# The last scaling and addition of a two-block kernel, shared between GpSimd and the vector engine, with the output stored in 768 and 256 KB

## The chip, the core and the metric

The kernel runs on one core of a Trainium2 chip. The metric is the device time of one execution in microseconds; the numbers given are the median of several executions. Besides the times there is one execution taken by the hardware profiler, with a page and a trace of it.

## What is computed

Two transformer-like blocks follow each other on a sequence of 256 tokens with 1024 features. The change touches only the last statement of the second block's second layer: the merged result `out` is normalised over its features, multiplied by a gain and a gate, and added to the residual `x`, which is then the result of the whole program.

```python
def rms_norm(x, g=None):
    xf = x.astype(jnp.float32)
    y = xf * lax.rsqrt(jnp.mean(xf * xf, axis=-1, keepdims=True) + EPS)
    if g is not None:
        y = y * g.astype(jnp.float32)
    return y.astype(x.dtype)

def second_block(x, c, ctx, c_ctx, w_mod, ...):
    ...
    for l in range(DEPTH_2):
        ...
        out = merge_branches(o_ret, o_mlp, o_diff, mlog_, w_branch_out[l], w_out[l])
        x = x + gate * rms_norm(out, g_post[l])
        ...
    return x
```

## The kernel before

All activations stand with the features on the 128 partitions. The residual is `h`, 8 tiles (`KT`) of 128 features by 256 tokens (`T`) in float32, 1 MB in all and 1 KB of each partition per tile. The weights come as a stream of units of 512 KB through a ring of four buffers, loaded by the queue of SyncE (`sp`, line 511 and, for the last three, line 514). ScalarE (`act`) makes the high part of a unit (line 1319), the vector engine (`dve`) the low part (line 468, `w_lo` = `ring` minus `w_hi`), and TensorE (`pe`) multiplies by both. Nothing is scheduled automatically: each engine's program is written out in order, and the engines wait for each other by counting semaphores.

The end of the program, which is what the change touches, runs as follows.

- For each of the 8 output tiles of the last product (`wo`), ScalarE squares the tile into `sq2` (line 1887) and writes the tile, scaled by the gate, into `unnormed` (line 1874; `unnormed` is a name for `diffz`, and `area` in the trace). The vector engine folds the squares together (line 1915), and TensorE sums them over the partitions (line 576).
- ScalarE turns the sum into `rstd`, 128 x 256, by a logarithm and an exponential (lines 1307 and 1308). The exponential raises the semaphore `out_rstd`, which the vector engine waits for.
- `add_out` (from line 2345) then works on pairs of tiles, 128 x 512 elements each. Line 2353 multiplies a pair of `unnormed` by `rstd`, repeated over the two tiles, and line 2356 adds the pair to `h`. The two kinds are interleaved, so that an addition never waits for the multiplication just before it: multiply 0, multiply 1, add 0, multiply 2, add 1, multiply 3, add 2, add 3. Each addition raises `resid_ready` by 2.
- SyncE stores `h[:, 0:4]` once two pairs are added (line 516), and `h[:, 4:8]` once all four are (line 518), 512 KB each. It then waits for both stores, and all engines meet at the end of the program (line 233).

GpSimd (`pool`) does a few small jobs earlier. Its last are the multiplications of line 2776, 128 x 256, in the middle of the second layer. It also runs the additions of line 2763, 128 x 512. Its helper `link` raises `pool_step` and waits for it, that is, it lets an instruction finish before the next one starts. The semaphore `pool_laid` has been raised three times by other lines of GpSimd before the end.

Of the kernel before, what the change touches and what calls it, by code (L numbers as in the profile page):

```python
# [14 lines left out]
ALU = mybir.AluOpType  # L15
# [6 lines left out]
P = 128  # L22
AREA = 25472
D = 1024
KT = D // P
T = 256
# [14 lines left out]
LAYERS = 2  # L41
# [144 lines left out]
RESID_BLOCK2 = 4 + 4 + KT + KT  # L186
# [18 lines left out]
def slot_units(l):  # L205

    return [(part, l, j) for part in SLOT_PARTS[l] for j in range(4)]
# [24 lines left out]
def two_block_kernel(nc, stream, mod_stream, cond, pack, pack2, bs_rows, x_in, ctx_in, out):  # L232
    with ExitStack() as es:
        def sb(name, shape, dt=F32):
            return es.enter_context(nc.sbuf_tensor(name, shape, dt))

        def sem(name):
            return es.enter_context(nc.semaphore(name))
# [13 lines left out]
        h = sb("h", [P, KT, T])  # L252
# [15 lines left out]
        rstd = sb("rstd", [P, 2 * T])  # L268
# [19 lines left out]
        def cut(*shape):  # L288
            n = int(np.prod(shape))
            v = area[:, Area.at:Area.at + n]  # L290
            Area.at += n
            if len(shape) == 2:
                v = v.rearrange("p (a b) -> p a b", a=shape[0])
            if len(shape) == 3:
                v = v.rearrange("p (a b c) -> p a b c", a=shape[0], b=shape[1])
            return v
# [59 lines left out]
        sp = cut(4, 16)  # L356
# [3 lines left out]
        def early_swapped(part, l):  # L360

            at = 2 + 2 * EARLY_ROPES[l].index(part)
            return aux[:, at:at + 2, :].rearrange("p a b -> p (a b)").rearrange("p (a b) -> p a b", b=T)

        def swaps(part):

            half = HD // 2 if part[0] == "d" else HD
            return [(to, to + half if to // half % 2 == 0 else to - half, half) for to in range(0, P, half)]
# [31 lines left out]
        unnormed = diffz  # L400
# [26 lines left out]
        resid_ready = sem("resid_ready")  # L427
# [3 lines left out]
        stored = sem("stored")  # L431
        S = {}

        def s(name):
            if name not in S:
                S[name] = sem(name)
            return S[name]
# [3 lines left out]
        def wait_taken(eng, name):  # L441

            _, _, who, count = BANK[name]
            eng.wait_ge(EV[who], count)
# [25 lines left out]
        def load_mod(eng, m, body=0, first=False):  # L470

            if not first:
                eng.wait_ge(s("mod_used"), m - 1 + body)
            eng.dma_start(mod_slot(m), mod_stream[m + body]).then_inc(s(f"mod_loaded{m % 2}"), 16)
# [20 lines left out]
        @block.sync  # L495
        def _(sp):
            sp.dma_start(h[:, :, :], x_in).then_inc(consts_loaded, 16)
            sp.dma_start(pk[:, 0:width(PACK)], pack[:, 0:width(PACK)]).then_inc(consts_loaded, 16)
            for u in range(RING):
                sp.dma_start(ring[:, u, PLACE:], stream[u]).then_inc(unit_loaded[u], 16)  # L500
            sp.dma_start(pk[:, width(PACK):width(PACK + PACK1)], pack[:, width(PACK):]).then_inc(block1_loaded, 16)
            for st in range(2):
                sp.dma_start(cond_silu(st), cond[:, st]).then_inc(s("cond_loaded"), 16)
            for m in range(2):
                load_mod(sp, m, first=True)
            rounds = NU // RING
            with sp.Fori(1, rounds) as r:
                for u in range(RING):

                    sp.wait_ge(units_multiplied, RING * r + (u + 1 - RING))  # L510
                    sp.dma_start(ring[:, u, PLACE:], stream[RING * r + u]).then_inc(unit_loaded[u], 16)
            for u in range(rounds * RING, NU):
                sp.wait_ge(units_multiplied, u + 1 - RING)
                sp.dma_start(ring[:, u % RING, PLACE:], stream[u]).then_inc(unit_loaded[u % RING], 16)
            sp.wait_ge(resid_ready, RESID_BLOCK2 + LAYERS * KT - KT // 2)
            sp.dma_start(out[:, 0:KT // 2, :], h[:, 0:KT // 2, :]).then_inc(stored, 16)
            sp.wait_ge(resid_ready, RESID_BLOCK2 + LAYERS * KT)
            sp.dma_start(out[:, KT // 2:KT, :], h[:, KT // 2:KT, :]).then_inc(stored, 16)
            sp.wait_ge(stored, 32)


# [1380 lines left out]
        def _(dve):  # L1902
# [8 lines left out]
            tt_, ts, stt = dve.tensor_tensor, dve.tensor_scalar, dve.scalar_tensor_tensor  # L1911
# [433 lines left out]
            def add_out(l, st, x, done, tiles):  # L2345

                before = outs_scaled[0] - tiles[0]
                outs_scaled[0] += len(tiles)
                v = slice(T * st, T * st + T)
                both = rstd[:, v].unsqueeze(1).broadcast_to([P, 2, T])  # L2350
                for k in range(tiles[0], tiles[0] + len(tiles) + 2, 2):
                    if k in tiles:
                        tt_(unnormed[:, k:k + 2, v], unnormed[:, k:k + 2, v], both, ALU.mult).then_inc(s("out_scaled"), 2)
                    if k - 2 in tiles:
                        dve.wait_ge(s("out_scaled"), before + k)
                        tt_(x[:, k - 2:k, :], x[:, k - 2:k, :], unnormed[:, k - 2:k, v], ALU.add).then_inc(done, 2)
# [133 lines left out]
            for l in range(LAYERS):  # L2490
# [178 lines left out]
                        fold(v, k, k - 1)  # L2669

                dve.wait_ge(s("out_rstd"), 1 + 2 * l)
                add_out(l, 0, h, resid_ready, range(KT))


        @block.gpsimd
        def _(pool):
# [8 lines left out]
            tt_, ts = pool.tensor_tensor, pool.tensor_scalar  # L2685
# [65 lines left out]
            def decay_tables(l, hh):  # L2751

                n = 4 * l + hh
                f, b = dmat[:, hh, :], aux[:, 9, :]
                three = lambda v: v.rearrange("p (a b) -> p a b", a=2)
                pool.wait_ge(s("decay_exp"), 2 * n + 1)
                link(pool.affine_select(out=three(f), in_=three(f), compare_op=ALU.is_ge, fill=0.0, base=0,
                                        pattern=[[-P, 2], [1, T]], channel_multiplier=-1))
                pool.wait_ge(s("decay_exp"), 2 * n + 2)
                pool.affine_select(out=three(b), in_=three(b), compare_op=ALU.is_ge, fill=0.0, base=0,  # L2760
                                   pattern=[[P, 2], [-1, T]], channel_multiplier=1).then_inc(s("decay_masked"), 1)
                pool.wait_ge(s("decay_masked"), 2 * n + 1)
                pool.tensor_tensor(f, f, b, ALU.add).then_inc(s("decay_masked"), 1)
# [20 lines left out]
            def swap_halves(part, l):  # L2784

                z, at = (diffz if part[0] == "d" else retz), (0 if part[1] == "k" else 4)
                dst = early_swapped(part, l) if part in EARLY_ROPES[l] else ring_swapped
                wait_taken(pool, (part, l, 3))
                for to, of, n in swaps(part):
                    pool.dma_start(dst[to:to + n, :, :], z[of:of + n, at:at + 4, 0:T]).then_inc(s(SWAPPED[part, l][0]), 16)  # L2790

            pool.wait_ge(block2_loaded, 16)
            for l in range(LAYERS):
                for part in EARLY_ROPES[l]:
                    if l == 1 and part == "dq":
                        pool.wait_ge(s("ctx_modulated"), LAYERS * KT)
                    swap_halves(part, l)
                for slot, name in enumerate(slot_units(l)):
                    for kind, step in SLOTS[l][slot]:
                        if kind == "tables":  # L2800
                            decay_tables(l, step)
                        if kind == "ret":
                            ret(l, step)
                    if name == ("rk", l, 3):
                        swap_halves("rk", l)
                    if name == ("rq", 0, 3):
                        pool.wait_ge(s("ring_roped"), RING_ROPED["rk", 0])
                        swap_halves("rq", l)

# [167 lines left out]
```

## Time and profile before

| what | us |
|---|---|
| median of 3 executions | 1491.61 |
| lowest and highest of them | 1489.47, 1491.94 |
| the profiled execution, its own time | 1491.69 |
| span of its trace | 1490.0 |

The profiled execution took 1.7 us more than the span of its trace, and it lies 0.08 us above the median. In the span TensorE was busy for 1445.0 us (97%), the vector engine for 957.8 us (64%), ScalarE for 721.5 us (48%) and GpSimd for 96.9 us (7%). These shares are means over a long program; the change lies in its last 8 us, where TensorE has already ended. So the end has to be read by itself, from the timeline and the chain of waits of the last microseconds.

### The profile page before, as it was taken

The page shows a single profiled execution, that of the slowest core. Times are in us where ns is not written, and L with a number is a line of the kernel's source. Part 1 is how long each engine was busy: PE and PEld are TensorE (multiplying, and loading weights), DVE is VectorE, ACT ScalarE, POOL GpSimd, SP SyncE. Part 2 cuts the span into 40 slices and gives each one's busy share as a digit, 9 for nine tenths or more (in the row PEclk, how much of TensorE's full clock was granted, in tenths as well). Part 3 has the DMA queues.
Part 4 walks back from the last instruction along what each step waited for, and adds up shares of the span by engine and source line. Part 5 has one row for each costly group of instructions (what it writes and reads, how often), then busy time and mean ns, then how long its engine had stood idle before and what let it go on. Part 6 is the DMA issues. An engine that isn't in the chain of part 4 may idle for free.

```text
span 1490.0 us, 25861 instructions
## 1 busy us (share of the span) xinstructions
PE 1445.0 (97%) x9976; PEld 1289.9 (87%) x9976; DVE 957.8 (64%) x1516; ACT 721.5 (48%) x1252; POOL 96.9 (7%) x153
## 2 busy tenths in 40 slices
PE   6999999989999999999999999999999999999997
PEld 6999999769999998877778788888889887889997
DVE  5888788677666678865654447654246745647665
ACT  5444466366444466336445353222245446556444
POOL 4700000000000000102001000000000103010000
PEclk9999999999999999999999999999999999999999
DMA  7766646516666644652222224533333542325663
GB/s 275 241 219 199 214 142 197 171 69 224 224 219 212 222 165 145 199 160 78 86 73 70 62 80 153 172 127 113 99 102 108 152 127 85 100 87 185 210 210 130
DMA packets 72440, 227.43 MB, mean 153 GB/s; under 512 B 7072, under 2 KB 21408, under 8 KB 71840
## 3 DMA queue, kind: packets, MB, share of 16 engines
q1 hardware_dynamic: 54528, 194.67, 40.4%
q10 hardware_dynamic: 16416, 27.34, 5.7%
q0 software_dynamic: 1408, 4.20, 1.2%
q8 instruction: 61, 1.00, 0.3%
q14 instruction: 27, 0.22, 0.1%
HBM read 220.94 MB, written 1.05 MB: 149 GB/s over the span
## 4 chain that ended last, share of the span: by engine, by line
PE 86%; DVE 5%; ACT 4%; DMA 3%; issue 2%; DVEq 0%; SPq 0%; ACTq 0%
PE ps L548 36%; PE ps L561 20%; PE ps L553 18%; DMA ring<-stream 2%; PE ps L576 2%; PE ps L1069 1%; ACT w_hi L1319 1%; PE ps L1085 1%; DVE w_lo L468 1%; PE ps L1077 1%; PE ps L1153 1%; PE ps L1142 1%; PE ps L1122 0%; DMA pk<-pack 0%; PE ps L1102 0%
## 5 line engine op out<-in xcount | busy, mean ns | idle before, releaser
L468 DVE TENSOR_TENSOR w_lo<-ring,w_hi 128x1024 fp32r<-128x1024 f32 (+1 forms) x347 | 414.7, 1201 | 269.0 <-ACT w_hi L1319 264.9
L1319 ACT ACTIVATE w_hi<-ring 128x1024 fp32r<-128x1024 f32 (+1 forms) x347 | 360.2, 1039 | 331.3 <-DMA ring<-stream 249.4
L548 PE MATMUL ps<-hn_hi,w_hi 128*128 128x256 f32 (+1 forms) x1720 | 494.7, 316 | 3.2 <-ACT area L1388 1.6
L548 PE MATMUL ps<-hn_lo,w_hi 128*128 128x256 f32 (+1 forms) x1720 | 486.2, 311 | 0.0
L548 PEld LDWEIGHTS ps<-hn_hi,w_hi 128*128 128x128 f32 x1720 | 324.3, 189 | 26.7 <-issue 5.6
L548 PEld LDWEIGHTS ps<-hn_lo,w_hi 128*128 128x128 f32 x1720 | 324.4, 189 | 19.3 <-issue 0.7
L553 PE MATMUL ps<-hn_hi,w_lo 128*128 128x256 f32 (+1 forms) x1720 | 291.8, 312 | 0.4 <-DVE w_lo L468 0.4
L553 PEld LDWEIGHTS ps<-hn_hi,w_lo 128*128 128x128 f32 x1720 | 247.5, 189 | 20.4 <-DVE w_lo L468 0.7
L1388 ACT ACTIVATE area<-ps 128x512 f32<-128x512 f32 (+1 forms) x136 | 67.1, 507 | 196.2 <-PE ps L553 182.2
L561 PE MATMUL ps<-area_r,w_hi 128*128 128x256 f32 (+1 forms) x578 | 131.8, 323 | 0.6 <-ACT area L1388 0.3
L561 PEld LDWEIGHTS ps<-area_r,w_hi 128*128 128x128 f32 x578 | 95.7, 188 | 10.7 <-DVE w_lo L468 0.9
L561 PE MATMUL ps<-area_r,w_lo 128*128 128x256 f32 (+1 forms) x289 | 92.6, 320 | 0.0
L548 PE MATMUL ps<-hid_hi,w_hi 128*128 128x256 f32 x352 | 83.0, 278 | 1.7 <-DVE hid_lo L2044 1.7
L548 PE MATMUL ps<-hid_lo,w_hi 128*128 128x256 f32 x352 | 82.6, 277 | 0.0
L561 PE MATMUL ps<-w_hi,hn_hi 128*128 128x512 f32 (+1 forms) x192 | 77.1, 402 | 0.0
L561 PE MATMUL ps<-w_lo,hn_hi 128*128 128x512 f32 (+1 forms) x192 | 73.4, 382 | 0.0
L561 PE MATMUL ps<-w_hi,hn_lo 128*128 128x512 f32 (+1 forms) x192 | 73.3, 382 | 0.0
L548 PEld LDWEIGHTS ps<-hid_hi,w_hi 128*128 128x128 f32 x352 | 66.1, 188 | 2.1 <-issue 1.0
L548 PEld LDWEIGHTS ps<-hid_lo,w_hi 128*128 128x128 f32 x352 | 66.3, 188 | 0.0
L561 PE MATMUL ps<-hn_hi,w_hi 128*128 128x256 f32 (+1 forms) x175 | 56.0, 320 | 5.0 <-DVE hn_lo L1926 2.9
L2790 POOL DMA_DIRECT2D area<-area x24 | 14.1, 595 | 686.3 <-ACT area L1388 686.3
L561 PEld LDWEIGHTS ps<-area_r,w_lo 128*128 128x128 f32 x289 | 54.3, 188 | 4.5
(331 smaller groups left out, 1843.9 us busy)
## 6 DMA issues: line engine op xcount, KB each, us to landing
ring<-stream SPq DMA_DIRECT2D x359, 512.0 KB, 3.9
mod_at<-mod_stream ACTq DMA_DIRECT2D x24, 512.0 KB, 5.6
area<-mod_stream ACTq DMA_DIRECT2D x22, 512.0 KB, 4.8
area<-area POOLq DMA_DIRECT2D x16, 128.0 KB, 4.7
area<-area POOLq DMA_DIRECT2D x8, 256.0 KB, 4.2
pk<-pack ACTq DMA_DIRECT2D x1, 1610.0 KB, 9.3
pk<-pack SPq DMA_DIRECT2D x1, 1549.0 KB, 12.3
h<-x_in SPq DMA_DIRECT2D x1, 1024.0 KB, 4.9
```

What stands on the lines that cost most here:

```text
L468: eng.tensor_tensor(lo[:, 0:w], raw, hi[:, 0:w].bitcast(F32), ALU.subtract).then_inc(lo_ready[who], 1)
L548: m = pe.matmul(dst, weights[0][wcols], x[n][xcols], start=(start and n == 0), stop=False, skip_group_check=True)
L553: return pe.matmul(dst, weights[1][wcols], x[0][xcols], start=False, stop=stop, skip_group_check=True)
L561: m = pe.matmul(dst, w_, x_, start=(start and n == 0), stop=(stop and n == 2), skip_group_check=True)
L576: m = pe.matmul(bank(b, 0, tokens), c("ones"), src, start=(k == first), stop=(k == KT - 1), skip_group_check=True)
L1069: pe.matmul(bank(4 + m_, T * st, 2 * T - T * st), diffz[rows, 4 + hh, q0:q0 + P], diffz[rows, hh, keys], start=True, stop=True).then_inc(s ...
L1077: m = pe.transpose(bank(6, P * kt, P), aux[:, 4 + n % 2, P * kt:P * kt + P], c("ident"))
L1085: m = pe.matmul(bank(7, P * qt, P), diffv[:, kt, P * hh:P * hh + P], aux[:, 6 + n % 2, P * kt:P * kt + P], start=(kt == 2 * st), stop=(kt ...
L1142: m = pe.matmul(bank(4 + n % 2, T * kt, T), retz[:, hh, T * st + P * kt:T * st + P * kt + P], retz[:, 4 + hh, T * st:T * st + T], start=(k ...
L1153: m = pe.matmul(bank(6 + n % 2, 0, T), retv[:, 2 * st + kt, P * hh:P * hh + P], aux[:, n % 2, T * kt:T * kt + T], start=(kt == 0), stop=(s ...
L1319: act.activation(w_parts(name)[0][:, 0:w], ring[:, u % RING, PLACE:PLACE + w], ACT.Copy).then_inc(hi_ready, 1)
L1388: act.activation(dst, bank(BANK[name][0], 0, tokens), func, **kw).then_inc(act_evac, 1)
```

## The change

GpSimd takes the first pair of tiles: at the end of its program it waits for `out_rstd`, multiplies the pair by `rstd`, waits until that is done (`link`), adds the pair to `h`, and raises `pool_laid` to 4. The vector engine's `add_out` runs over tiles 2 to 7 in the second layer, three pairs in place of four. The first store now takes tiles 0 to 5, 768 KB, once GpSimd is done and the vector engine has added two pairs; the second takes tiles 6 and 7, 256 KB, once the third pair is added.

```diff
-            sp.wait_ge(resid_ready, RESID_BLOCK2 + LAYERS * KT - KT // 2)
-            sp.dma_start(out[:, 0:KT // 2, :], h[:, 0:KT // 2, :]).then_inc(stored, 16)
-            sp.wait_ge(resid_ready, RESID_BLOCK2 + LAYERS * KT)
-            sp.dma_start(out[:, KT // 2:KT, :], h[:, KT // 2:KT, :]).then_inc(stored, 16)
+            sp.wait_ge(s("pool_laid"), 4)
+            sp.wait_ge(resid_ready, RESID_BLOCK2 + LAYERS * KT - 4)
+            sp.dma_start(out[:, 0:KT - 2, :], h[:, 0:KT - 2, :]).then_inc(stored, 16)
+            sp.wait_ge(resid_ready, RESID_BLOCK2 + LAYERS * KT - 2)
+            sp.dma_start(out[:, KT - 2:KT, :], h[:, KT - 2:KT, :]).then_inc(stored, 16)
             sp.wait_ge(stored, 32)
...
-                add_out(l, 0, h, resid_ready, range(KT))
+                add_out(l, 0, h, resid_ready, range(KT) if l == 0 else range(2, KT))
...
+            pool.wait_ge(s("out_rstd"), 3)
+            link(tt_(unnormed[:, 0:2, 0:T], unnormed[:, 0:2, 0:T], rstd[:, 0:T].unsqueeze(1).broadcast_to([P, 2, T]), ALU.mult))
+            tt_(h[:, 0:2, :], h[:, 0:2, :], unnormed[:, 0:2, 0:T], ALU.add).then_inc(s("pool_laid"), 1)
```

Two lists show what each engine has in a row. In them a name like `area` or `h` is the tensor written, and what stands behind the arrow is read. The change puts one line into the SyncE part, so that later lines have numbers one higher: 2353 and 2354 are the same multiplication, 2356 and 2357 the same addition.

The vector engine's last instructions before the change:

```order
L1915 TENSOR_TENSOR area<-area 128x256 [waits folded,squares_ready] x3
L2353 TENSOR_TENSOR area<-area,rstd 128x2x256 [waits out_rstd]
L2353 TENSOR_TENSOR area<-area,rstd 128x2x256
L2356 TENSOR_TENSOR h<-h,area 128x512 [waits out_scaled]
L2353 TENSOR_TENSOR area<-area,rstd 128x2x256
L2356 TENSOR_TENSOR h<-h,area 128x512 [waits out_scaled]
L2353 TENSOR_TENSOR area<-area,rstd 128x2x256
L2356 TENSOR_TENSOR h<-h,area 128x512 [waits out_scaled] x2
```

And after it:

```order
L1916 TENSOR_TENSOR area<-area 128x256 [waits folded,squares_ready] x3
L2354 TENSOR_TENSOR area<-area,rstd 128x2x256 [waits out_rstd]
L2354 TENSOR_TENSOR area<-area,rstd 128x2x256
L2357 TENSOR_TENSOR h<-h,area 128x512 [waits out_scaled]
L2354 TENSOR_TENSOR area<-area,rstd 128x2x256
L2357 TENSOR_TENSOR h<-h,area 128x512 [waits out_scaled] x2
L233 UNCONDITIONAL_BRANCH
```

One multiplication and one addition have left this engine, and the order of the rest is the same.

GpSimd's last instructions before the change:

```order
L2776 TENSOR_TENSOR area<-area 128x256 [waits state_decay,ret_out]
L2776 TENSOR_TENSOR area<-area 128x256
L2776 TENSOR_TENSOR area<-area 128x256 [waits state_decay,ret_out]
L2776 TENSOR_TENSOR area<-area 128x256
L233 UNCONDITIONAL_BRANCH
```

And after it:

```order
L2777 TENSOR_TENSOR area<-area 128x256 [waits state_decay,ret_out]
L2777 TENSOR_TENSOR area<-area 128x256
L2812 TENSOR_TENSOR area<-area,rstd 128x2x256 [waits out_rstd]
L2813 TENSOR_TENSOR h<-h,area 128x512 [waits pool_step]
L233 UNCONDITIONAL_BRANCH
```

The two instructions stand behind all of GpSimd's other work, and nothing is queued behind them.

## Rows read from the trace of the kernel before

**Rows 1.** The chain that ended last, from 1470 us: start, length, what.

```profile
1469.92 9.86 PE ps L561 x87
...
1481.50 0.42 ACT rstd L1308
...
1482.01 0.75 DVE area L2353 x2
...
1485.72 0.06 DVE h L2356
```

**Rows 2.** Timeline of the last stretch: start, length, engine, line, output<-inputs, count.

```profile
1481.50 0.42 ACT L1308 ACTIVATE rstd<-lnr 128x256 f32<-128x256 f32 x1
1482.01 1.29 DVE L2353 TENSOR_TENSOR area<-area,rstd 128x512 f32<-128x512 f32 x2 [4.08 <-ACT rstd L1308]
1483.22 0.69 DVE L2356 TENSOR_TENSOR h<-h,area 128x512 f32<-128x512 f32 x1
1483.83 0.68 DVE L2353 TENSOR_TENSOR area<-area,rstd 128x512 f32<-128x512 f32 x1
1484.43 0.68 DVE L2356 TENSOR_TENSOR h<-h,area 128x512 f32<-128x512 f32 x1
1485.03 0.69 DVE L2353 TENSOR_TENSOR area<-area,rstd 128x512 f32<-128x512 f32 x1
1485.14 0.35 SPq L516 DMA_DIRECT2D out<-h  x1
1485.63 1.29 DVE L2356 TENSOR_TENSOR h<-h,area 128x512 f32<-128x512 f32 x2
1486.95 0.34 SPq L518 DMA_DIRECT2D out<-h  x1
```

**Rows 3.** Windows: stretch, length, busy of each engine, PEclk, DMA share, GB/s.

```profile
1485.95:1486.00 0.05, 0.00 (x0) 0.00 (x0) 0.05 (x1) 0.00 (x0) 0.00 (x0) 0.50 0.60 246
1486.00:1487.00 1.00, 0.00 (x0) 0.00 (x0) 0.92 (x2) 0.00 (x0) 0.00 (x0) 0.50 1.02 410
1487.30:1487.70 0.40, 0.00 (x0) 0.00 (x0) 0.00 (x0) 0.00 (x0) 0.00 (x0) 0.50 0.01 0
1487.75:1487.80 0.05, 0.00 (x0) 0.00 (x0) 0.00 (x0) 0.00 (x0) 0.00 (x0) 0.50 1.02 410
1489.05:1489.10 0.05, 0.00 (x0) 0.00 (x0) 0.00 (x0) 0.00 (x0) 0.00 (x0) 0.50 0.27 82
```

**Rows 4.** GpSimd's large additions and multiplications, then the last additions: duration ns min/median/max.

```profile
L2763 POOL TENSOR_TENSOR area<-area x8: 1285/1287/1292, 682.8 to 1254.7; 128x512 f32<-128x512 f32 x8
L2776 POOL TENSOR_TENSOR area<-area x16: 722/738/1232, 808.7 to 1329.1; 128x256 f32<-128x256 f32 x16
L2356 DVE TENSOR_TENSOR h<-h,area x4: 684/684/685, 1483.2 to 1486.2; 128x512 f32<-128x512 f32 x4
```

**Rows 5.** Timeline where both engines read two tensors at once, in both layers.

```profile
808.71 1.44 POOL L2776 TENSOR_TENSOR area<-area 128x256 f32<-128x256 f32 x2 [69.05 <-ACT area L1683]
809.55 1.68 DVE L468 TENSOR_TENSOR w_lo<-ring,w_hi 128x1024 fp32r<-128x1024 f32 x1 [2.84 <-ACT w_hi L1319]
810.58 1.23 POOL L2776 TENSOR_TENSOR area<-area 128x256 f32<-128x256 f32 x1 [0.43 <-ACT area L1683]
...
812.88 1.22 DVE L468 TENSOR_TENSOR w_lo<-ring,w_hi 128x1024 fp32r<-128x1024 f32 x1
...
1309.26 1.70 DVE L468 TENSOR_TENSOR w_lo<-ring,w_hi 128x1024 fp32r<-128x1024 f32 x1 [0.51 <-ACT w_hi L1319]
```

**Rows 6.** Timeline of the early stage, where the vector engine has work back to back.

```profile
38.04 2.36 DVE L468 TENSOR_TENSOR w_lo<-ring,w_hi 128x1024 fp32r<-128x1024 f32 x2
...
38.33 1.00 POOL L2698 TENSOR_SCALAR area<-area 128x16 f32<-128x16 f32 x1
39.41 1.11 POOL L2699 TENSOR_SCALAR area<-area 128x16 f32<-128x16 f32 x1
40.60 0.26 POOL L2689 TENSOR_SCALAR area<-area 128x16 f32<-128x16 f32 x1
```

**Rows 7.** GpSimd's slowest instruction of this size.

```profile
68.81 2.59 POOL L2746 TENSOR_SCALAR area<-pk 128x512 f32<-128x512 f32 x1
```

## The prediction

> **What bounds the kernel now.** The first view to read is the chain that ended last, in its last 20 us [rows 1]. TensorE's last weight products end at 1479.78 us, and from the moment ScalarE has `rstd` at 1481.92 us only the vector engine and then the store carry the time. So a change here can neither disturb nor use TensorE; what counts is when the output has landed.
>
> The second view is the timeline [rows 2]. The vector engine starts at 1482.01 us, 0.09 us behind `rstd`, and runs 8 instructions. The starts of neighbours lie 0.60 us apart (1483.83, 1484.43, 1485.03, 1485.63), each lasts 0.68, so each begins 0.08 us before its forerunner is done. The last ends at 1486.92 us. SyncE issues the first store at 1485.14 us, 0.03 us behind the second addition, and the second store at 1486.95 us, 0.03 us behind the last.
>
> The third view is the windows of the DMA engines [rows 3]. Data of the first store flows from 1485.96 us, 0.82 us behind its issue, at 410 GB/s; at that rate 512 KB (524,288 bytes) take 1.28 us. From 1487.30 to 1487.70 us nothing flows. The second store flows from 1487.75 us, 0.80 us behind its issue, to about 1489.07 us. The span ends at 1489.96 us, printed as 1490.0, so 0.9 us lie between the last data and the end. The stores are thus limited by their issue, with a gap of half a microsecond between them that better timing could close.
>
> **The change part by part.**
>
> *The vector engine loses two instructions.* By itself that takes 2 x 0.60 = 1.21 us off its part [rows 2]: six instructions end at 1482.01 + 5 x 0.605 + 0.68 = 1485.72 us. The first of its additions that count for the first store (its second, pair 2) would end at 1485.11 us, which is where the second addition ended before.
>
> *GpSimd gains two instructions.* The nearest rows are its eight additions of 128 x 512, all 1.29 us [rows 4]. The new multiplication has the same size, but reads `rstd` repeated over two rows of 256, for which the trace has no example on this engine; I take 1.29 us for it too, since the multiplications of one row of 256 take 0.74 us each, and two of them 1.47. After a pause of 69 us the first instruction of line 2776 was no slower than the next (two in 1.44 us) [rows 5], so I charge nothing for a late wake-up. It would start at about 1482.0 us, as the vector engine does, and alone end at 1482.0 + 1.29 + 0.08 + 1.29 = 1484.7 us, before the 1485.11 us of the vector engine. If the engines did not touch each other, its work would be hidden.
>
> *Do they touch each other?* Here the trace has rows for what the diff does not show [rows 5]. In both layers a vector-engine subtraction of 128 x 1024 started while GpSimd was multiplying. It took 1.68 us and 1.70 us where undisturbed it takes 1.22. In the first case GpSimd was busy until 808.71 + 1.44 = 810.15 us and the subtraction had started at 809.55, so 0.60 us of overlap cost it 0.46. The other way round, GpSimd's multiplication at 810.58 us met the subtraction that ended at 811.23: 0.65 us of overlap, and 1.23 us in place of 0.74, so 0.49 lost. In both directions the one that came second lost the whole overlap but some 0.15 us. That is not a mild slowing: one of the two stands still. The early stage says who comes next [rows 6]: two subtractions stand back to back from 38.04 to 40.40 us, and GpSimd's tiny instructions (0.26 us undisturbed) take 1.00 and 1.11 us there, the first ending at 39.33 us, when the first subtraction ended (38.04 + 1.22). So a waiting GpSimd instruction gets its turn between two vector instructions, even when the next of these is at hand.
>
> The six multiplications and additions left on the vector engine and the two on GpSimd all read two tensors in SBUF. So they should stand in one line: each of GpSimd's costs the vector engine 1.29 - 0.14 = 1.15 us, whichever starts first, since the vector engine has work for the whole time. Its end is then 1485.72 + 2 x 1.15 = 1488.0 us, which is 1.1 us later than before, and its last-but-one addition ends 0.60 us ahead of that, at 1487.4 us. GpSimd, also held up, is done by about 1485.5 us, so its semaphore is not what the store waits for.
>
> The Trainium skill, in the page "SBUF — State Buffer", section "Who interferes with whom", states it as a rule: a vector instruction with two SBUF inputs and a GpSimd instruction that reads SBUF exclude each other, and the later one is blocked until the earlier is done. By that rule the change moves work that costs 0.60 us an instruction to where it costs about twice as much on the same line. The trace agrees, with the 0.46 and 0.49 us above.
>
> *The stores.* The first now waits for the vector engine's second addition. In the one-line case it is issued at 1487.43 us, and the second, at 1488.0 + 0.03, can't be earlier than 0.35 us behind it (the length of an issue) and isn't. Data flows from 1487.43 + 0.82 = 1488.25 us. The 768 KB take 1.92 us and the 256 KB, already queued, 0.64: 1 MB at 410 GB/s is 2.56 us, so the last data comes at 1490.81 us, and the end 0.9 us later at 1491.7 us. Before, the end was at 1489.96. **The sum is +1.75 us**: +1.1 from the vector engine's later end, and +0.65 because the first store is issued 2.3 us later than before, so that the two run behind each other with nothing of the first done ahead; the smaller second store returns less than that costs. No row has a store with 2 KB or 6 KB per partition; I take both at the rate of the 4 KB ones. If the small one ran at half the rate that would be +0.6 us, and if its start overlapped perfectly, nothing.
>
> *Everything else* is at nothing: the semaphore traffic is one more wait on SyncE, which waits anyway; behind GpSimd's new wait nothing is queued; TensorE's lower granted clock of 0.50 in the last 4 us [rows 3] moves no step of the vector engine, whose distances stay at 0.60 us across it [rows 2].
>
> **The rivals.**
>
> *They do not block each other.* The vector engine ends at 1485.72 us, the first store is issued at 1485.14 us as before, the second at 1485.75. The data would then run without a gap from 1485.96 for 2.56 us to 1488.52, where it ended at 1489.07 before: a gain of 0.55 us, not 1.2, since the DMA engines are then full. This gives 1491.1 us. Rows 5 and 6 speak against it, with every overlap that I find; for it speaks only that no row has these two shapes together.
>
> *GpSimd's instructions are much longer than its additions of the same size.* Its only multiplication by a constant with broken-up rows, 128 x 512 in rows of 32, took 2.59 us [rows 7], part of it probably blocked too. If the repeated `rstd` or the pitch of `unnormed` made both new instructions that long, the vector engine, standing in line, would end 2 x 1.30 = 2.6 us later still: +4.35 us, 1496.0 us, which is slower. It becomes slower by more than 0.2% once the two together take 3.8 us in place of 2.6. Against it: rows of 256 cost line 2776 no more per element than expected from line 2763.
>
> *The wait for GpSimd decides.* It would do so in the first rival if GpSimd took over 1.5 us each, 0.4 us in all behind the addition. Then each 0.1 us is passed on to the first store, hardly to the end; about 1491.3 us. This is where the change would not do what it says.
>
> **How the numbers follow.** The profiled execution took 1491.69 us, 0.08 above the median; with +1.75 it is 1493.4, and against the median 1493.3 us, which I predict. One in line: 0.78. No blocking: 0.12. Long GpSimd instructions: 0.06. GpSimd's wait: 0.04. The runs of before spread over 2.5 us, more than the whole effect, and a time within 0.2% (3 us) is about what can't be told from no change. The range is 1490.9 to 1494.8 us: at the low end the rival without blocking, at the high end GpSimd instructions of 1.9 us or a slow small store together with some scatter. Slower by over 0.2% gets 0.11 (the long instructions, and the forecast of +1.75 with 1.3 us of scatter above it), faster 0.02, within 0.2% 0.87.
>
> **What the profile of the changed kernel would show.** Right: between 1482 and 1488 us, two vector instructions with about 1.8 us in place of 0.68 and one or both of GpSimd's longer than 1.29; the end of the vector engine near 1488.0; stores issued at 1487.4 and 1488.0 with data without a gap for 2.56 us. Wrong: all six vector instructions at 0.68 us and stores at 1485.14 and 1485.75 (they don't block), or a GpSimd instruction over 2 us with no vector instruction inside it (its own length). If the vector engine ends at 1488.0 us but the span does not grow, the stores' part is wrong.

## The result: 1493.92 us, and the profile after

The changed kernel takes 1493.92 us in the median of 22 executions, the kernel before 1491.52 us in the median of 22 on the same occasions. The ratio is 1.0015 with a 95% interval of 1.0008 to 1.0022: clear of no change, but within 0.2% of it at the best estimate. Forecast were 1493.3 us, range 1490.9 to 1494.8, and "within 0.2%". Single executions of one kernel spread over several microseconds (before from 1489.47 to 1495.92), so the two profiled executions, 1491.69 and 1494.77 us, must not simply be subtracted: the changed kernel's `rstd` was ready 1.14 us later than before (1483.06 in place of 1481.92), with no edit ahead of it but the numbering of lines. The end is therefore read from the end of the exponential that gives `rstd`; counted from there, the span ended at +8.04 us before and ends at +9.98 us now. (The expectations below still give +9.90 and a rise of 1.86 for the changed kernel; its span of 1493.04 us makes them +9.98 and +1.94.) The medians differ by 2.40 us, and the interval reaches from 1.2 to 3.3 us, so the 1.94 us of the traces agree with it but are known more closely.

The timeline of the changed kernel, the last stretch without TensorE (start, length, engine, line, output<-inputs), answers to [rows 2]:

```profile
1482.64 0.42 ACT L1309 ACTIVATE rstd<-lnr 128x256 f32<-128x256 f32 x1
1483.13 1.26 POOL L2812 TENSOR_TENSOR area<-area,rstd 128x512 f32<-128x512 f32 x1 [151.70 <-ACT rstd L1309]
1483.16 3.45 DVE L2354 TENSOR_TENSOR area<-area,rstd 128x512 f32<-128x512 f32 x2 [4.18 <-ACT rstd L1309]
1484.47 1.59 POOL L2813 TENSOR_TENSOR h<-h,area 128x512 f32<-128x512 f32 x1
1486.53 0.68 DVE L2357 TENSOR_TENSOR h<-h,area 128x512 f32<-128x512 f32 x1
1487.13 0.68 DVE L2354 TENSOR_TENSOR area<-area,rstd 128x512 f32<-128x512 f32 x1
1487.73 1.28 DVE L2357 TENSOR_TENSOR h<-h,area 128x512 f32<-128x512 f32 x2
1488.49 0.35 SPq L517 DMA_DIRECT2D out<-h  x1
1489.04 0.34 SPq L519 DMA_DIRECT2D out<-h  x1
```

The two multiplications of the vector engine take 3.45 us, where two took 1.29 in [rows 2]. The first of them alone:

```profile
1483.16 1.78 DVE L2354 TENSOR_TENSOR area<-area,rstd 128x512 f32<-128x512 f32 x1 [4.18 <-ACT rstd L1309]
```

GpSimd was first, by 0.03 us. The vector engine's four later instructions, with GpSimd done at 1486.06 us, are at 0.68 us again. The vector engine ends at 1489.01 us, +5.95 from `rstd`, where it ended at +5.00 before.

What SyncE waited for says which engine the stores hang on (engine and line, what it waited for, us, times, longest):

```profile
SPq L516 <- DVE h L2357: 18.8, 1, 18.8
SPq L233 <- DMA out<-h: 3.3, 1, 3.3
SPq L519 <- DVE h L2357: 0.2, 1, 0.2
```

It is the vector engine both times, not GpSimd, and after the last issue SyncE waits 3.3 us for the output to land (2.3 us before). The windows of the DMA engines (stretch, length, the engines' busy time, clock, DMA share, GB/s) answer to [rows 3]:

```profile
1489.30:1491.10 1.80, 0.00 (x0) 0.00 (x0) 0.00 (x0) 0.00 (x0) 0.00 (x0) 0.50 1.03 416
1491.10:1491.90 0.80, 0.00 (x0) 0.00 (x0) 0.00 (x0) 0.00 (x0) 0.00 (x0) 0.50 0.92 353
1491.90:1492.00 0.10, 0.00 (x0) 0.00 (x0) 0.00 (x0) 0.00 (x0) 0.00 (x0) 0.50 0.48 164
```

Data starts at 1489.30 us, 0.81 behind the first issue, and flows without a gap until 1491.97 us, slower in its last quarter. The gap of [rows 3] is gone, but all of the megabyte now lies behind the late first issue.

### The profile page after: what moved, and what is told of

Read it like the earlier page. It is cut to its first block, busy times and chain, and to the rows that moved or that the text cites. A ratio compares the mean times of both kernels' runs of the same rounds, so it can differ in the third digit from the quotient of the medians.

```text
span 1493.0 us, 25861 instructions
## 1 busy us (share of the span) xinstructions
PE 1444.8 (97%) x9976; PEld 1289.7 (86%) x9976; DVE 958.6 (64%) x1514; ACT 721.4 (48%) x1252; POOL 98.5 (7%) x155
## 3 DMA queue, kind: packets, MB, share of 16 engines
HBM read 220.94 MB, written 1.05 MB: 149 GB/s over the span
## 4 chain that ended last, share of the span: by engine, by line
PE 87%; DVE 5%; ACT 3%; DMA 2%; issue 2%; DVEq 0%; SPq 0%; ACTq 0%
PE ps L549 36%; PE ps L562 21%; PE ps L554 18%; DMA ring<-stream 2%; PE ps L577 1%; PE ps L1070 1%; ACT w_hi L1320 1%; PE ps L1086 1%; DVE w_lo L468 1%; PE ps L1078 1%; PE ps L1154 1%; PE ps L1143 1%; PE ps L1123 0%; DMA pk<-pack 0%; PE ps L1103 0%
```

## Experiments

The theory is the forecast's, one line: a vector instruction that reads two tensors in SBUF (the memory where activations and weights stand) and a GpSimd instruction that reads SBUF exclude each other, which makes the vector engine later; and the first store, held back until three quarters are ready, adds to it. The rivals are that the loss is the stores' alone, that it is GpSimd's own slowness, or that any activity of GpSimd disturbs. All readings are from the end of `rstd`; "last store" is the time from its issue to the end of the span. Each row is read from one trace, so a difference of a few hundredths says little; the one kernel that was traced twice, with two pairs on GpSimd, ended at +10.90 and +10.91. Whole times are compared only for the kernels of which the text says "timed".

| kernel | vector engine done | first, last issue | span ends | last store |
|---|---|---|---|---|
| before | +5.00 | +3.22, +5.03 | +8.04 | 3.01 |
| changed | +5.95 | +5.43, +5.98 | +9.98 | 4.00 |
| split of the stores alone | +5.00 | +4.43, +5.03 | +8.97 | 3.94 |
| GpSimd alone, 512 and 512 KB | +5.96 | +4.23, +5.98 | +9.00 | 3.02 |
| GpSimd writes only | +3.80 | +3.28, +3.83 | +7.81 | 3.98 |
| GpSimd copies | +6.34 | +5.82, +6.37 | +10.36 | 3.99 |
| GpSimd takes two pairs | +6.88 | +6.36, +6.91 | +10.90 | 3.99 |
| before, four stores | +5.00 | +2.02, +5.02 | +7.81 | 2.79 |
| before, 512, 256, 256 KB | +5.01 | +3.23, +5.03 | +7.96 | 2.93 |
| `rstd` in PSUM | +4.39 | +2.16, +4.42 | +7.33 | 2.91 |

### The two halves of the change, each alone

The split alone is the kernel before with

```diff
-            sp.wait_ge(resid_ready, RESID_BLOCK2 + LAYERS * KT - KT // 2)
-            sp.dma_start(out[:, 0:KT // 2, :], h[:, 0:KT // 2, :]).then_inc(stored, 16)
+            sp.wait_ge(resid_ready, RESID_BLOCK2 + LAYERS * KT - 2)
+            sp.dma_start(out[:, 0:KT - 2, :], h[:, 0:KT - 2, :]).then_inc(stored, 16)
             sp.wait_ge(resid_ready, RESID_BLOCK2 + LAYERS * KT)
-            sp.dma_start(out[:, KT // 2:KT, :], h[:, KT // 2:KT, :]).then_inc(stored, 16)
+            sp.dma_start(out[:, KT - 2:KT, :], h[:, KT - 2:KT, :]).then_inc(stored, 16)
```

> The kernel before with one part of the change alone: stores of 768 and 256 KB, all four pairs still on the vector engine. All times are counted from the end of the exponential that gives rstd (the kernel before: vector engine done at +5.00, span ends at +8.04; the change: +5.95 and +9.90). Both theories, engines in one line and GpSimd merely too slow, expect the vector engine done at +5.00; the first store is issued behind the third addition at +4.4, 1 MB flows without a gap from +5.2 to +7.8 or +7.9, and the span ends at +8.8. If the split costs nothing, as one would think from its smaller last store, it ends at +7.6 or below.

Measured: the vector engine is done at +5.00 and the span ends at +8.97, 0.17 us above the +8.8 expected and 0.93 us later than before, so the split costs time without any help of GpSimd's. Its vector instructions are as before; the issues have moved together, and nothing of the output has gone out ahead (timeline, then windows):

```profile
1485.92 1.28 DVE L2356 TENSOR_TENSOR h<-h,area 128x512 f32<-128x512 f32 x2
1486.63 0.34 SPq L516 DMA_DIRECT2D out<-h  x1
1487.23 0.34 SPq L518 DMA_DIRECT2D out<-h  x1
```

```profile
1487.40:1488.40 1.00, 0.00 (x0) 0.00 (x0) 0.00 (x0) 0.00 (x0) 0.00 (x0) 0.50 0.95 393
1488.40:1489.30 0.90, 0.00 (x0) 0.00 (x0) 0.00 (x0) 0.00 (x0) 0.00 (x0) 0.50 1.10 437
1489.30:1490.00 0.70, 0.00 (x0) 0.00 (x0) 0.00 (x0) 0.00 (x0) 0.00 (x0) 0.50 0.89 339
```

The other half is the changed kernel with even stores:

```diff
             sp.wait_ge(s("pool_laid"), 4)
-            sp.wait_ge(resid_ready, RESID_BLOCK2 + LAYERS * KT - 4)
-            sp.dma_start(out[:, 0:KT - 2, :], h[:, 0:KT - 2, :]).then_inc(stored, 16)
+            sp.wait_ge(resid_ready, RESID_BLOCK2 + LAYERS * KT - 6)
+            sp.dma_start(out[:, 0:KT // 2, :], h[:, 0:KT // 2, :]).then_inc(stored, 16)
             sp.wait_ge(resid_ready, RESID_BLOCK2 + LAYERS * KT - 2)
-            sp.dma_start(out[:, KT - 2:KT, :], h[:, KT - 2:KT, :]).then_inc(stored, 16)
+            sp.dma_start(out[:, KT // 2:KT, :], h[:, KT // 2:KT, :]).then_inc(stored, 16)
```

> The change with its other part alone: GpSimd takes the first pair, but the stores are 512 and 512 KB again, the first once GpSimd is done and the vector engine has added pair 1. Counted from the end of rstd. Engines in one line: vector engine done at +5.95 as in the change, first store issued at +4.2, second at +6.0, span ends at +9.0, so that about half of the change's +1.86 is the engines' and half is the stores'. If all of the loss were the stores' split, the span would end at +8.0; if all were the engines', at +9.9.

Measured: vector engine +5.96, issues +4.23 and +5.98, end +9.00, as expected by one line to 0.03 us. The four kernels form a square: GpSimd's part adds 0.96 us under even stores and 1.01 under uneven ones, the split adds 0.93 and 0.98. Each half of the change loses about a microsecond, and the halves add up.

### What in GpSimd's work holds up the vector engine

GpSimd only writes:

```diff
-            link(tt_(unnormed[:, 0:2, 0:T], unnormed[:, 0:2, 0:T], rstd[:, 0:T]...broadcast_to([P, 2, T]), ALU.mult))
-            tt_(h[:, 0:2, :], h[:, 0:2, :], unnormed[:, 0:2, 0:T], ALU.add).then_inc(s("pool_laid"), 1)
+            link(pool.memset(aux[:, 0:3, :], 0.0))
+            pool.memset(aux[:, 3:6, :], 0.0).then_inc(s("pool_laid"), 1)
```

> The change with GpSimd's two instructions replaced by two memsets of 128x1536 on tiles that nobody reads any more, some 1.4 us each; the first pair is left unscaled and not added. GpSimd is as busy as in the change and only reads nothing. If the two engines exclude each other over the reading of SBUF, the six vector instructions take 0.68 us each and are done at +3.8 from the end of rstd, and the span ends at +7.5. If it is GpSimd's being at work, or its writing, that holds up the vector engine, two of the six take 1.7 us or more and the end is at +5.9 or later.

Measured: the vector engine runs as if alone, +3.80 as expected, though GpSimd is busy from 1483.83 to 1486.64 us (timeline):

```profile
1483.83 1.38 POOL L2812 MEMSET area<- 128x1536 f32 x1 [152.09 <-ACT rstd L1309]
1483.87 1.29 DVE L2354 TENSOR_TENSOR area<-area,rstd 128x512 f32<-128x512 f32 x2 [4.18 <-ACT rstd L1309]
1485.08 0.68 DVE L2357 TENSOR_TENSOR h<-h,area 128x512 f32<-128x512 f32 x1
```

The span ended at +7.81, not +7.5: the first issue came 0.08 us behind the second addition, the megabyte flowed for 2.7 us in place of 2.56, and 1.05 us passed behind the last data in place of 0.9. The kernel leaves the first pair unscaled and not added, as the next one does.

GpSimd copies, that is, it reads one tensor:

```diff
-            link(tt_(unnormed[:, 0:2, 0:T], unnormed[:, 0:2, 0:T], rstd[:, 0:T]...broadcast_to([P, 2, T]), ALU.mult))
-            tt_(h[:, 0:2, :], h[:, 0:2, :], unnormed[:, 0:2, 0:T], ALU.add).then_inc(s("pool_laid"), 1)
+            for n in range(2):
+                pool.tensor_copy(aux[:, 0:3, :], aux[:, 3:6, :]).then_inc(s("pool_laid"), 1) if n else link(pool.tensor_copy(aux[:, 6:9, :], aux[:, 3:6, :]))
```

> As the run with two memsets, but with two copies of 128x1536 on tiles that nobody reads any more: GpSimd reads one tensor and writes one. The first pair is left unscaled and not added. If it is enough that GpSimd reads SBUF, each copy (1.04 us for 1024 elements in the trace of before, so about 1.5) costs the vector engine its length less 0.15: done at +3.8 + 2.7 = +6.5 from the end of rstd. If GpSimd must read two tensors, the vector engine is done at +3.8 as with the memsets.

Measured: the two multiplications take 3.83 us in place of 1.29, and the vector engine is done at +6.34, where +6.5 was expected.

```profile
1480.05 3.33 POOL L2813 COPY area<-area 128x1536 f32<-128x1536 f32 x2 [152.06 <-ACT rstd L1309]
1480.09 3.83 DVE L2354 TENSOR_TENSOR area<-area,rstd 128x512 f32<-128x512 f32 x2 [4.08 <-ACT rstd L1309]
```

So what holds up these vector instructions, which read two tensors in SBUF, is the reading of SBUF by GpSimd, of one tensor or two, and not its writing or its being at work. The copies touch none of the tensors that the vector engine reads, so a shared tensor is not needed for it. The Trainium skill, page "SBUF — State Buffer", section "Who interferes with whom", draws the line in the same place, between GpSimd instructions that read SBUF and those that only write; both runs agree with it, with 2.54 us lost to the copies and none to the memsets.

Twice the dose: GpSimd takes pairs 0 and 1 (the edit against the changed kernel, long lines cut short).

```diff
-            sp.wait_ge(s("pool_laid"), 4)
-            sp.wait_ge(resid_ready, RESID_BLOCK2 + LAYERS * KT - 4)
+            sp.wait_ge(s("pool_laid"), 5)
+            sp.wait_ge(resid_ready, RESID_BLOCK2 + LAYERS * KT - 6)
...
-            sp.wait_ge(resid_ready, RESID_BLOCK2 + LAYERS * KT - 2)
+            sp.wait_ge(resid_ready, RESID_BLOCK2 + LAYERS * KT - 4)
...
-            link(tt_(unnormed[:, 0:2, 0:T], ...
-            tt_(h[:, 0:2, :], ...
+            for k in (0, 2):
+                link(tt_(unnormed[:, k:k + 2, 0:T], ...
+                tt_(h[:, k:k + 2, :], ...
...
-                add_out(l, 0, h, resid_ready, range(KT) if l == 0 else range(2, KT))
+                add_out(l, 0, h, resid_ready, range(KT) if l == 0 else range(4, KT))
```

> The dose doubled: GpSimd takes two pairs (four instructions), the vector engine the other two; the first store waits for all of GpSimd and for pair 2. In one line: 4 x 0.60 + 4 x 1.15 + 0.2, so the later of the two engines is done at +7.2 from the end of rstd, the stores issue at about +6.7 and +7.2 and the span ends at +11.1. If they don't exclude each other: vector engine done at +2.6, GpSimd at +5.5 (4 x 1.29 and three gaps of 0.08), span end at about +9.9.

Measured: the vector engine is done at +6.88 and the span ends at +10.90, 0.3 and 0.2 us less than the sum of the expectation; by the rival without exclusion the vector engine would have been done at +2.6. The timeline shows the two taking turns:

```profile
1484.06 1.26 POOL L2813 TENSOR_TENSOR area<-area,rstd 128x512 f32<-128x512 f32 x1 [152.72 <-ACT rstd L1309]
1484.09 3.45 DVE L2354 TENSOR_TENSOR area<-area,rstd 128x512 f32<-128x512 f32 x2 [4.18 <-ACT rstd L1309]
1485.40 1.59 POOL L2814 TENSOR_TENSOR h<-h,area 128x512 f32<-128x512 f32 x1
1486.95 1.70 POOL L2813 TENSOR_TENSOR area<-area,rstd 128x512 f32<-128x512 f32 x1
1487.46 3.41 DVE L2357 TENSOR_TENSOR h<-h,area 128x512 f32<-128x512 f32 x2
1488.74 1.59 POOL L2814 TENSOR_TENSOR h<-h,area 128x512 f32<-128x512 f32 x1
```

GpSimd's second instruction is at hand from 1485.40 us while the vector engine's first multiplication runs to 1484.09 + 1.78 = 1485.87. The overlap of 0.47 us costs it 0.33 (1.59 in place of 1.26), 0.14 less than the overlap, as in [rows 5]. After that the two engines take strict turns to the end, one instruction each.

The same kernel, timed:

> The doubled dose once more, now timed, to see whether what is read from the last microseconds of a trace is what the clock of the whole program shows. In the trace the end lies 2.86 us later than before (+10.90 in place of +8.04), so the ratio should be 1.0019 if the rest of the program is untouched. If the loss were partly outside the tail, more.

Measured: 1494.20 against 1491.07 us, ratio 1.0022, interval 1.0013 to 1.0031; the expected 1.0019 lies inside. Its trace ends at +10.91. So what the last microseconds show is what the whole program's time shows, within the scatter, and there is no sign of a loss elsewhere.

### Can the end be made shorter than before?

The kernel before with four stores in place of the two (only the new lines are shown, here and in the next edit):

```diff
+            for n in range(4):
+                sp.wait_ge(resid_ready, RESID_BLOCK2 + (LAYERS - 1) * KT + 2 * n + 2)
+                sp.dma_start(out[:, 2 * n:2 * n + 2, :], h[:, 2 * n:2 * n + 2, :]).then_inc(stored, 16)
+            sp.wait_ge(stored, 64)
```

> The kernel before, with four stores of 256 KB, each as soon as its pair is added. The vector engine is done at +5.00 from the end of rstd as before; the last store has only 256 KB behind the last addition: data until +6.5, span end at +7.4, 0.65 us less than before. Timed, that is 1490.9 us beside 1491.5. If each further store costs the DMA queue something of its own, the end stays at +8.0.

Measured: +7.81, 0.23 us less than before and not 0.65; timed, 1490.87 against 1490.89 us, ratio 1.0000 (0.9991 to 1.0008), no difference that can be told. The data (windows):

```profile
1486.50:1487.10 0.60, 0.00 (x0) 0.00 (x0) 0.00 (x0) 0.00 (x0) 0.00 (x0) 0.50 0.95 352
1487.10:1487.80 0.70, 0.00 (x0) 0.00 (x0) 0.00 (x0) 0.00 (x0) 0.00 (x0) 0.50 1.03 386
1487.90:1488.00 0.10, 0.00 (x0) 0.00 (x0) 0.00 (x0) 0.00 (x0) 0.00 (x0) 0.50 0.21 62
```

The stores of 256 KB, 2 KB from each partition, flow at 350 to 390 GB/s and not at 410, and after the last data (1487.93 us) 1.15 us pass until the span ends at 1489.08, where it was 0.9 before.

The kernel before with three stores, 512, 256 and 256 KB:

```diff
+            for a, b in ((0, 4), (4, 6), (6, 8)):
+                sp.wait_ge(resid_ready, RESID_BLOCK2 + (LAYERS - 1) * KT + b)
+                sp.dma_start(out[:, a:b, :], h[:, a:b, :]).then_inc(stored, 16)
+            sp.wait_ge(stored, 48)
```

> The kernel before with stores of 512, 256 and 256 KB. Counted from the end of rstd: vector engine done at +5.00. Four stores of 256 KB ended the span at +7.81, 512 and 512 KB at +8.04, 768 and 256 KB at +8.97. If what counts is how much is left to send behind the last addition and how well the queue is fed, this one ends like the four stores, at +7.7 to +7.8; if a mixture of sizes costs by itself, later than +8.04.

Measured: +7.96, between what the two readings wanted: worse than the 7.7 to 7.8 expected and still under +8.04. Its windows show data without a gap from 1487.5 us, 0.8 behind the first issue, to about 1490.2. So here the first issue sets the end, at +3.23 where the four stores had +2.02. A mixture of sizes was no loss against 512 and 512 KB; the late first store of the change is one.

The last attempt takes GpSimd's help without its price: `rstd` is written to PSUM, the memory where TensorE's sums stand, the four multiplications come first, and GpSimd only adds pair 0. The output goes out in four stores of 256 KB. (The edit against the kernel before, its main lines; `dst` is where ScalarE's exponential writes.)

```diff
+            sp.wait_ge(s("pool_laid"), 4)
+            sp.dma_start(out[:, 0:2, :], h[:, 0:2, :]).then_inc(stored, 16)
+            for n in range(1, 4):
+                sp.wait_ge(resid_ready, RESID_BLOCK2 + (LAYERS - 1) * KT + 2 * n)
+                sp.dma_start(out[:, 2 * n:2 * n + 2, :], h[:, 2 * n:2 * n + 2, :]).then_inc(stored, 16)
+            sp.wait_ge(stored, 64)
...
-                root(6, bank(7, 0, T), T, sumsq_ready, (7, 11)[l], D, s("out_rstd"))
+                root(6, bank(7, 0, T), T, sumsq_ready, (7, 11)[l], D, s("out_rstd"), dst=None if l == 0 else bank(7, T, T))
...
+                    both = bank(7, T, T).unsqueeze(1).broadcast_to([P, 2, T])
+                    for k in range(0, KT, 2):
+                        tt_(unnormed[:, k:k + 2, 0:T], unnormed[:, k:k + 2, 0:T], both, ALU.mult).then_inc(s("out_scaled"), 2)
+                    for k in range(2, KT, 2):
+                        dve.wait_ge(s("out_scaled"), 2 * KT + k + 2)
+                        tt_(h[:, k:k + 2, :], h[:, k:k + 2, :], unnormed[:, k:k + 2, 0:T], ALU.add).then_inc(resid_ready, 2)
...
+            pool.wait_ge(s("out_scaled"), 2 * KT + 2)
+            tt_(h[:, 0:2, :], h[:, 0:2, :], unnormed[:, 0:2, 0:T], ALU.add).then_inc(s("pool_laid"), 1)
```

> An attempt at a version that beats both, and a test of one line: ScalarE writes rstd to PSUM, so that the vector engine's four multiplications read only one tensor from SBUF; they run first, GpSimd adds pair 0 behind the first of them, then the vector engine adds pairs 1 to 3; four stores of 256 KB. If only two readers of SBUF exclude each other, GpSimd's addition costs the vector engine nothing (all seven at about 0.68 us), which is done at +4.4 from the end of rstd, and the span ends at +6.9, 1.2 us less than before: 1490.3 us beside 1491.5. If any GpSimd instruction blocks, one of the multiplications takes 1.8 us, the vector engine is done at +5.6 and the span ends at +8.0.

Measured: nothing is blocked (timeline):

```profile
1489.81 2.48 DVE L2678 TENSOR_TENSOR area<-area,ps 128x512 f32<-128x512 f32 x4 [4.15 <-ACT ps L1309]
1490.58 1.26 POOL L2820 TENSOR_TENSOR h<-h,area 128x512 f32<-128x512 f32 x1 [153.51 <-DVE area L2678]
1492.21 1.89 DVE L2681 TENSOR_TENSOR h<-h,area 128x512 f32<-128x512 f32 x3
```

The vector engine's multiplications now read one tensor from SBUF and one from PSUM. Four of them take 2.48 us, that is 0.60 apart, and GpSimd's addition falls inside them at its bare 1.26. The vector engine is done at +4.39 and the span ends at +7.33, 0.71 us less than before; 1.2 was expected, and the missing 0.4 to 0.5 is again the small stores'. Of the 0.71 us, 0.23 is what four stores gave the kernel before by themselves (+7.81), so that the new order of the work is worth 0.48. (This trace is of an execution of 1498.77 us, the slowest of the 12. Its `rstd` was ready only at 1489.71 us, so that its extra time lies ahead of the stretch read here.) Timed: 1490.98 against 1490.89 us, ratio 1.0001 (0.9990 to 1.0012). 0.71 us is 0.05% of this program, less than the interval. Its last stretch is the shortest of all; that the whole kernel is faster is not shown.

## Why the prediction was right, point by point

- **What bounds the end.** Right: the vector engine and then the stores. No term of the loss was found elsewhere. The time alone would not have shown this: the stated range of 3.9 us also holds the median of the kernel before. What bears the forecast out are the steps counted from `rstd`.
- **The engines stand in one line.** Right. Forecast was an end of the vector engine 1.10 us later than before, measured 0.95. GpSimd's instructions held it up by 2.15 us in all (+5.95 beside the +3.80 with memsets) and not 2.30. Of the 0.15 too much, 0.06 is their length, 1.26 us and not the 1.29 of [rows 4], and 0.03 is GpSimd's earlier start; the rest is in hundredths of the overlaps. That only two of the six would be long, at about 1.8 us, was right as well: the first took 1.78.
- **Repeated `rstd` on GpSimd.** No dearer than an addition: 1.26 us. The rival of long GpSimd instructions falls with that. Why the instruction of [rows 7] took 2.59 us was not tried and stays open.
- **The store does not wait for GpSimd.** Right: GpSimd was done at +3.00, the first store went at +5.43. Forecast for GpSimd was 1485.5 us, which is +3.6: too late by 0.6, without effect.
- **The stores.** The mechanism was right, its size too small: +0.65 was forecast, and the square gives 0.93 to 0.98. Two terms were mis-sized, by 0.3 us together. One is "at the rate of the 4 KB ones": the megabyte took 2.67 us and not 2.56, its last quarter flowing at 353 GB/s. The other is the time behind the last data, 1.07 us in place of 0.9. A smaller one is the issue: the first store went 0.08 us behind its addition, where the sum had 0.03. It was 0.08 in all four kernels in which a wait for GpSimd stands ahead of that for the addition and the addition comes last; that the second wait is the reason is not shown.
- **The sum.** +1.75 forecast, +1.94 in the trace; 1493.3 us forecast, 1493.92 measured. The engines' 0.15 too much and the 0.3 too little for the stores' data and landing partly cancelled, which is luck. Of the 0.6 us between the two times only 0.2 are explained by the last stretch; the rest is within the scatter of the medians.
- **The rival without blocking** would have needed all vector instructions at 0.68 us. The run with memsets shows what it would have looked like, and also that its price was too friendly: with 768 and 256 KB its span ends at +7.81, a gain of 0.23 and not of 0.55.

## What to carry to other kernels

Before work is given to an idle engine, look for a row of the trace in which both engines run: here two stretched subtractions of 1.7 us said that the help would be queued in front of the work it was to relieve, and at twice the price. Help was free in these runs only where GpSimd read nothing from SBUF (the memsets), or where the vector instruction read only one tensor from it, as the multiplications with `rstd` in PSUM did. Of the stores that end this program, what counts is how much has gone out before the last result is there; making the last one smaller by making the first one later and larger was a loss of 0.93 to 0.98 us.

## What the runs showed of the hardware

- A store's end does not follow its size alone. The last store of 512 KB took 3.01 and 3.02 us from its issue to the end of the span, one of 256 KB behind other small ones 2.79 to 2.93: half the data saved some 0.1 to 0.2 us, where the data itself needs 0.6 us less. The small stores flow more slowly (350 to 390 GB/s in place of 410), and 1.05 to 1.2 us pass behind their last data in place of 0.9. In all three kernels the data of the last store follows that of the store ahead without a gap, so part of the 2.79 to 2.93 us may be a wait for it. Whether the 2 KB per partition or the number of stores is the reason was not tried and stays open.
- Being shut out costs the later instruction its overlap less about 0.15 us: 0.46 and 0.49 us for 0.60 and 0.65 in [rows 5], 0.33 for 0.47 here.
- Released by the same semaphore, GpSimd and the vector engine started 0.02 to 0.04 us apart, GpSimd first, in all six traces in which both wait for `rstd`. How the sum would come out with the vector engine first no trace shows.
